# Compressed attention units of the second mixer: transposes three steps after their scores, first value product one step later

## The chip, the cores and the metric

The kernel runs on one core of one Trainium2 chip. The metric is the device time of one execution in microseconds. The core has TensorE (PE, its weight loads PEld), VectorE (DVE), ScalarE (ACT) and GpSimd (POOL), each with a queue of its own that is worked off in the order in which the program was written, and DMA queues. Engines wait for each other by semaphores.

## The reference, cut to what matters

The program is a block of several branches followed by a second block of two layers on a sequence of 1024 tokens of width 1024. The first layer of the second block has a mixer with three kinds of attention over the same queries, 8 heads in 2 groups of 4:

```
o_cmp, p_cmp = compressed_branch(q, kcmp, vcmp, slopes)   # 63 compressed tokens
idx = selection_indices(p_cmp, s)                         # per group, from p_cmp.sum over heads
o_sel = selected_branch(q, kv_heads(ks), kv_heads(vs), idx, slopes)
o_win = window_branch(q, kv_heads(kw), kv_heads(vw), slopes)
o = g[..., 0:1] * o_cmp + g[..., 1:2] * o_sel + g[..., 2:3] * o_win

# compressed_branch
logits = einsum('bgrtd,bgnd->bgrtn', q, kc) - slopes * dist
p = softmax(where(dist >= 0, logits, NEG)) * valid
o = einsum('bgrtn,bgnd->bgrtd', p, vc)
```

The window and selected branches are the same pattern with wider rows: scores, a bias by distance, exponentials, a product with the values, and a division by the row sum at the end. Only the compressed branch divides its probabilities before its value product, since their sum over heads also feeds the selection.

## The kernel before, in words

The attention of this mixer is cut into eight blocks of 128 queries, taken from the last (i = 7) to the first (i = 0). A block has 18 units: two compressed ones (kind "cmp", g = 0 and 1, four heads each, 4 x 63 columns), eight window units and eight selected units (kind "soft", one head each). A window unit is up to 640 keys wide (five blocks of 128; four or fewer from i = 3 on), a selected one up to 1024.

Each engine runs its own loop over steps, and a unit passes through them. In what follows S, T, C, P and O with a number stand for work of a block's unit of that number (0 and 1 are the compressed units, 2 the first window unit, 3 the second; -2 and -1 are the last two selected units of the block before).

- PE, per step: the scores S of the unit of this step (L1429 for cmp, L1435 for soft); the transposes T of the unit of two steps ago (L1453), 128 columns each; then value products: C0 for the first compressed unit three steps after its scores and C1 for the second five steps after (L1473), P for a pair of soft units (L1484); and O, the transposes of a finished group's output (L1494). L1503 are the transposes of a finished block.
- DVE, per step: the bias on the scores and the row minimum (L2866 cmp, L2875 soft); for a compressed unit of the step before the normalization, whose result T waits for (L2885, L2888, L2889, semaphore c_normed, then L2891, a sum over heads); the addition of finished outputs (L2902 for cmp; L2907, L2908 and four L2910 for soft); a part of the selection (L2630 to L2641) in six of the window steps.
- ACT, per step: the copies of transposed rows from PSUM to SBUF (L2112); the exponentials (L2098 cmp, L2102 soft); four steps after the last unit of a group the copy of its output (L2118), which O waits for.

T writes one of two PSUM banks in turn, so a transpose of piece t waits (n_copied) until ACT has copied piece t - 2. A row of more than four blocks of 128 has two pieces. C1 waits until DVE has added the output of group 1 of the block before (o_taken). The order on each engine is what the loops write; there is no planner. S of unit n waits until the bank it writes is free: for i of 4 and more that is after the bias of unit n - 2.

Of the kernel before, what the change touches and what calls it, by code (L numbers as in the profile page):

```python
# [67 lines left out]
def build(nc, x, c, w_mod, b_mod, g_pre, g_post, w_in, m_conv_w, m_conv_b, m_wq, m_wk, m_b_i, m_b_f,  # L68
# [5 lines left out]
    with ExitStack() as ctx:  # L74
# [437 lines left out]

        NSA_ORDER = list(range(TB - 1, -1, -1))

        def nsa_table():

            units, banks, pieces, turns, rows = [], [0] * 4, 0, 0, 0
            for o, i in enumerate(NSA_ORDER):
                for br, kind in enumerate(("cmp", "win", "sel")):
                    for h in range(0, N_H, 4 if kind == "cmp" else 1):  # L520
                        un = Unit()
                        un.kind, un.br, un.i, un.o, un.h, un.g, un.n = kind, br, i, o, h, h // 4, len(units)
                        un.b0 = max(0, i - 4) if kind == "win" else 0
                        un.blocks = 2 if kind == "cmp" else i + 1 - un.b0
                        un.w = 256 if kind == "cmp" else P * un.blocks
                        wide = 2 if i >= 4 else 1
                        bank_ = (un.n * wide) % 4
                        un.at = 512 * bank_
                        un.bank_free = max(banks[bank_:bank_ + wide])
                        banks[bank_:bank_ + wide] = [un.n + 1] * wide  # L530
                        un.first, un.last = un.h % 4 == 0, kind == "cmp" or un.h % 4 == 3
                        un.pieces = [(a, min(4, un.blocks - a)) for a in range(0, un.blocks, 4)]
                        un.piece = pieces
                        pieces += len(un.pieces)
                        un.row = rows
                        rows += kind != "cmp"
                        units.append(un)
            last_of = [max(un.n for un in units if un.o == o) for o in range(TB)]
            turn_of = []
            for step in range(len(units) + 10):  # L540
                if 0 <= step - 2 < len(units):
                    units[step - 2].turn = turns
                    turns += len(units[step - 2].pieces)
                if step - 8 in last_of:
                    turn_of.append(turns)
                    turns += 1
            soft = [un for un in units if un.kind != "cmp"]
            return units, soft, last_of, turn_of

        nsa_units, nsa_soft, nsa_last, nsa_turn = nsa_table()  # L550
        N_NSA = len(nsa_units)
# [416 lines left out]
        def _(pe):  # L968
# [471 lines left out]
            def n_turns(un):  # L1440

                if un.kind == "cmp":
                    pe.wait_ge(s.c_normed, 2 * un.o + un.g + 1)
                    row = crow[:, un.g, :]
                else:
                    pe.wait_ge(s.n_exp, un.row + 1)
                    row = ht[:, 4 + un.row % 4, :]
                for m, (a, blocks) in enumerate(un.pieces):
                    t = un.turn + m
                    if t >= 2:  # L1450
                        pe.wait_ge(s.n_copied, t - 1)
                    for b in range(blocks):
                        last = pe.transpose(ps[:, 2048 + 512 * (t % 2) + P * b:2048 + 512 * (t % 2) + P * b + P],  # L1453
                                            row[:, P * (a + b):P * (a + b) + P], ident[:, :])
                    last.then_inc(s.n_turned, 1)
# [12 lines left out]
            def c_values(un):  # L1468

                o = out_free(un)  # L1470
                pe.wait_ge(s.n_copied, un.turn + 1)
                for b in range(2):
                    last = mm(o[:, P * b:P * b + P], piece_of(un, b), vb[:, un.g, :], start=b == 0, stop=True,  # L1473
                              skip_group_check=True)
                last.then_inc(s.n_summed, 1)
# [32 lines left out]
            for step in range(N_NSA + 9):  # L1508
                if step < N_NSA:
                    n_scores(nsa_units[step])  # L1510
                if 0 <= step - 2 < N_NSA:
                    n_turns(nsa_units[step - 2])
                if at(step - 3, "cmp") and nsa_units[step - 3].g == 0:
                    c_values(nsa_units[step - 3])
                if at(step - 5, "cmp") and nsa_units[step - 5].g == 1:
                    c_values(nsa_units[step - 5])
                if at(step - 3, "soft") and nsa_units[step - 3].h % 2:
                    pair_values(nsa_units[step - 4], nsa_units[step - 3])
                if at(step - 5, "soft") and nsa_units[step - 5].last:
                    turned_out(nsa_units[step - 5])  # L1520
                if step - 8 in nsa_last:
                    n_heads(nsa_last.index(step - 8))
# [201 lines left out]
        def _(a):  # L1724
# [380 lines left out]
            def n_copies(un):  # L2105

                for m, (_, blocks) in enumerate(un.pieces):
                    t, p_ = un.turn + m, un.piece + m
                    a.wait_ge(s.n_turned, t + 1)
                    if p_ >= 8:  # L2110
                        a.wait_ge(s.n_summed, p_ - 7)
                    f(pt[:, 512 * (p_ % 8):512 * (p_ % 8) + P * blocks],  # L2112
                      ps[:, 2048 + 512 * (t % 2):2048 + 512 * (t % 2) + P * blocks], ACT.Copy).then_inc(s.n_copied, 1)
# [4 lines left out]
                f(out_t[:, un.g, :], bank(6 + un.g)[:, 0:256], ACT.Copy).then_inc(s.o_turned_in, 1)  # L2118

            for step in range(N_NSA + 9):  # L2120
                if 0 <= step - 2 < N_NSA:
                    n_copies(nsa_units[step - 2])
                if step < N_NSA:
                    n_exps(nsa_units[step])
                if step == N_NSA:
                    a.dma_start(xt[:, :, :], x_kept).then_inc(s.x_back, 16)
                if 0 <= step - 4 < N_NSA and nsa_units[step - 4].kind != "cmp" and nsa_units[step - 4].last:
                    out_taken(nsa_units[step - 4])
                if step - 8 in nsa_last:
                    i = nsa_last.index(step - 8)  # L2130
                    t = nsa_turn[i]
                    a.wait_ge(s.n_turned, t + 1)
                    f(no[:, :, P * NSA_ORDER[i]:P * NSA_ORDER[i] + P],
                      bank(4 + t % 2).rearrange("p (c t) -> p c t", c=4), ACT.Copy).then_inc(s.n_copied, 1)
# [217 lines left out]
        def _(v):  # L2352
# [563 lines left out]

            def outs_at(step):

                for n in (step - 4, step - 6):
                    if 0 <= n < N_NSA and nsa_units[n].last:  # L2920
                        un = nsa_units[n]
                        if n == step - 4 - 2 * (un.kind != "cmp" or un.g == 1):
                            n_outs(un)

            for step in range(N_NSA + 7):
# [632 lines left out]
```

## Time and profile before

| | us |
|---|---|
| runs (three) | 2985.83, 2989.27, 2983.74; median 2985.83 |
| profiled execution | 2981.65 |
| its span, first to last instruction | 2979.9 |
| PE busy | 2792.1 (94%) |
| DVE busy | 2028.3 (68%) |
| ACT busy | 1181.8 (40%) |
| mean granted TensorE clock | 0.97 |

The attention of the second mixer, the only place that the change touches, runs from about 902 to 1197 us of the span. The profile's slices 13 to 16 lie in it; PE is at 8 or 9 tenths there, DVE at 6 or 7. Shares of busy time say which engine is the fullest over the whole stretch, and not which one is late at a given place; for that the trace is read at one border between two blocks.

### The profile page before, as it was taken

The page shows a single profiled execution, that of the slowest core. Times are in us where ns is not written, and L with a number is a line of the kernel's source. Part 1 is how long each engine was busy: PE and PEld are TensorE (multiplying, and loading weights), DVE is VectorE, ACT ScalarE, POOL GpSimd, SP SyncE. Part 2 cuts the span into 40 slices and gives each one's busy share as a digit, 9 for nine tenths or more (in the row PEclk, how much of TensorE's full clock was granted, in tenths as well). Part 3 has the DMA queues.
Part 4 walks back from the last instruction along what each step waited for, and adds up shares of the span by engine and source line. Part 5 has one row for each costly group of instructions (what it writes and reads, how often), then busy time and mean ns, then how long its engine had stood idle before and what let it go on. Part 6 is the DMA issues. An engine that isn't in the chain of part 4 may idle for free.

```text
span 2979.9 us, 39880 instructions
## 1 busy us (share of the span) xinstructions
PE 2792.1 (94%) x15515; PEld 2271.9 (76%) x15515; DVE 2028.3 (68%) x3468; ACT 1181.8 (40%) x2129; POOL 82.4 (3%) x152
## 2 busy tenths in 40 slices
PE   3999999678998988999999999989989999999999
PEld 3868885467787876778888888878757788888887
DVE  5443417669536666478777777779984877776885
ACT  3333317543326776343333344421153433333444
POOL 1000000210040000000000000000000000000000
PEclk8999999999999998999999999999989999999999
DMA  7101200023200000333223383311002333335632
GB/s 308 36 25 29 64 24 15 5 75 112 64 26 1 1 1 1 134 102 117 105 105 108 126 293 96 92 43 50 23 16 74 104 106 113 113 113 201 219 99 99
DMA packets 185701, 256.29 MB, mean 86 GB/s; under 512 B 29575, under 2 KB 138539, under 8 KB 181035
## 3 DMA queue, kind: packets, MB, share of 16 engines
q1 hardware_dynamic: 181520, 232.45, 23.7%
q10 hardware_dynamic: 3995, 21.30, 1.8%
q8 instruction: 124, 2.03, 0.3%
q14 instruction: 62, 0.51, 0.1%
HBM read 186.62 MB, written 67.11 MB: 85 GB/s over the span
## 4 chain that ended last, share of the span: by engine, by line
PE 55%; DVE 3%; ACT 1%; DMA 0%; issue 0%; DVEq 0%; ACTq 0%
PE ps L1597 27%; PE ps L1605 14%; PE ps L1552 10%; PE ps L1661 2%; PE ps L1712 1%; PE ps L1698 0%; DMA ring<-in_ffn_w_gate_dram 0%; PE ps L1002 0%; DVE sc L2443 0%; DVE h_low L2447 0%; DVE w_ring L2974 0%; ACT big L2322 0%; ACT h_high L2340 0%; ACT sc L2343 0%; DVE x_ops L3084 0%
## 5 line engine op out<-in xcount | busy, mean ns | idle before, releaser
L1597 PE MATMUL ps<-x_ops,w_ring 128*128 128x512 f32 x3696 | 840.3, 389 | 6.3 <-ACT even_rows L2223 3.1
L1597 PEld LDWEIGHTS ps<-x_ops,w_ring 128*128 128x128 f32 x3696 | 693.2, 188 | 151.5 <-issue 7.8
L1605 PE MATMUL ps<-a_ring,w_ring 128*128 128x512 f32 x1848 | 419.6, 389 | 0.0
L1605 PEld LDWEIGHTS ps<-a_ring,w_ring 128*128 128x128 f32 x1848 | 346.7, 188 | 72.6 <-DVE w_ring L2974 0.7
L1552 PE MATMUL ps<-h_high,ring_parts 128*128 128x512 f32 x1024 | 320.3, 394 | 17.9 <-DVE h_low L2447 9.2
L2165 ACT ACTIVATE w_ring<-ring 128x512 fp32r<-128x512 f32 x230 | 144.1, 628 | 300.6 <-PE ps L1597 284.8
L1552 PEld LDWEIGHTS ps<-h_high,ring_parts 128*128 128x128 f32 x1024 | 193.4, 190 | 63.0 <-issue 12.7
L2456 DVE TENSOR_TENSOR ring_parts<-ring,ring_parts 128x1024 fp32r<-128x1024 f32 (+2 forms) x77 | 91.6, 1190 | 209.8 <-ACT ring_parts L1799 209.2
L1552 PE MATMUL ps<-h_low,ring_parts 128*128 128x512 f32 x512 | 200.7, 392 | 0.0
L1799 ACT ACTIVATE ring_parts<-ring 128x1024 fp32r<-128x1024 f32 (+2 forms) x77 | 76.0, 989 | 275.5 <-PE ps L1552 175.3
L2974 DVE TENSOR_TENSOR w_ring<-ring,w_ring 128x512 fp32r<-128x512 f32 x230 | 157.8, 686 | 38.8 <-ACT w_ring L2165 38.8
L2178 ACT ACTIVATE a_ring<-a_raw 128x512 fp32r<-128x512 f32 x150 | 94.6, 630 | 206.9 <-PE ps L1605 174.6
L2979 DVE TENSOR_TENSOR a_ring<-a_raw,a_ring 128x512 fp32r<-128x512 f32 x150 | 103.6, 691 | 95.0 <-ACT a_ring L2178 94.6
L1110 PE MATMUL ps<-h_high,ring_parts 128*128 128x512 f32 (+1 forms) x384 | 121.0, 396 | 6.8 <-DVE hin_low L2464 5.6
L1381 PE MATMUL ps<-h_high,ring_parts 128*128 128x512 f32 x384 | 121.7, 399 | 5.5 <-DVE nin_low L2745 4.2
L2165 ACT ACTIVATE w_ring<-late 128x512 fp32r<-128x512 f32 x100 | 62.9, 629 | 150.3 <-PE ps L1597 150.3
L1552 PEld LDWEIGHTS ps<-h_low,ring_parts 128*128 128x128 f32 x512 | 97.3, 190 | 20.4
L2112 ACT ACTIVATE sc<-ps 128x512 f32<-128x512 f32 (+3 forms) x208 | 87.9, 457 | 56.1 <-PE ps L1453 55.5
L1453 PE MATMUL ps<-ident,ht 128*128 128x128 f32 x560 | 92.1, 287 | 17.7 <-DVE ht L2889 17.0
L2102 ACT ACTIVATE ht<-ht,stat 128x640 f32<-128x640 f32 (+7 forms) x128 | 94.1, 736 | 26.7 <-DVE stat L2875 26.0
L1435 PE MATMUL ps<-kt,qt 128*128 128x512 f32 (+3 forms) x384 | 102.9, 380 | 0.0
L1147 PE MATMUL ps<-h_high,ring_parts 128*128 128x512 f32 (+1 forms) x288 | 94.6, 410 | 0.9 <-DVE ring_parts L2456 0.9
(478 smaller groups left out, 4636.6 us busy)
## 6 DMA issues: line engine op xcount, KB each, us to landing
a_raw<-act_kept SPq DMA_DIRECT2D x70, 512.0 KB, 3.8
act_kept<-even_rows SPq DMA_DIRECT2D x12, 1536.0 KB, 5.1
act_kept<-odd_rows SPq DMA_DIRECT2D x10, 1536.0 KB, 5.1
ring<-in_ffn_w_gate_dram SPq DMA_DIRECT2D x12, 1024.0 KB, 5.8
ring<-in_ffn_w_up_dram SPq DMA_DIRECT2D x12, 1024.0 KB, 6.0
ring<-in_conv_w_pw_dram SPq DMA_DIRECT2D x24, 512.0 KB, 3.9
late<-in_ffn_w_gate_dram SPq DMA_DIRECT2D x10, 1024.0 KB, 5.8
late<-in_ffn_w_up_dram SPq DMA_DIRECT2D x10, 1024.0 KB, 6.0
```

What stands on the lines that cost most here:

```text
L1110: last = mm(o[0:m, 512 * half:512 * half + 512], w(wp_, k), hin[rp_][:, k, 512 * half:512 * half + 512], start=k == 0 and p_ == 0, stop=k ...
L1147: last = mm(bank(o)[0:m, :], w(wp_, k), hin[rp_][:, k, 512 * (f % 2):512 * (f % 2) + 512], start=k == 0 and p_ == 0, stop=k == KC - 1 and ...
L1381: last = mm(o[:, 512 * half:512 * half + 512], w(wp_, k), nin_parts[rp_][k][:, 512 * half:512 * half + 512], start=k == 0 and p_ == 0, sto ...
L1435: last = mm(ps[:, un.at + a:un.at + a + e], q, kt[:, 4 * (un.br - 1) + 2 * part_ + un.g, k0:k0 + e], start=part_ == 0, stop=part_ == 1)
L1552: last = mm(bank(banks + half), (hi, lo)[wp_][:, k, :], h_part[rp_][:, k, 512 * half:512 * half + 512], start=k == order[0][0] and p_ == 0 ...
L1597: last = mm(o, w_ring[:, i % 4, wp_, P * k:P * k + P], x_ops[:, X_OP[p], rp_, k, :], start=p in "176" and k == 0 and p_ == 0, stop=k == 3 ...
L1605: last = mm(bank(OUT_BANK[DOWN_GROUP[p] + c_]), w_ring[:, (A_UNITS + b) % 4, wp_, P * c_:P * c_ + P], a_ring[:, b % 4, rp_, :], start=p in ...
L2102: f(row, row, ACT.Exp, bias=r[:, 0:1], scale=-1.0, accum_out=row_sums[:, un.row % 16:un.row % 16 + 1]).then_inc(s.n_exp, 1)
L2165: f(unit_part(i, 0), unit_raw(i), ACT.Copy).then_inc(s.u_hi, 1)
L2178: f(a_ring[:, b % 4, 0, :], x_down_raw(b), ACT.Copy).then_inc(s.x_hi, 1)
L2974: tt(unit_part(i, 1), unit_raw(i), unit_part(i, 0).bitcast(F32), sub).then_inc(s.u_split, 1)
L2979: tt(a_ring[:, b % 4, 1, :], x_down_raw(b), a_ring[:, b % 4, 0, :].bitcast(F32), sub).then_inc(s.x_split, 1)
```

## The change

The new function turned_in names the units whose transposes belong to a step: a compressed unit three steps after its scores, a soft one two steps after as before. The table of turns, PE's loop (n_turns) and ACT's loop (n_copies) use it. So in the step of unit 2 nothing is transposed, in that of unit 3 the first compressed unit, and in that of unit 4 the second compressed unit and unit 2. C0 comes four steps after its scores instead of three; C1 stays where it was. On DVE the addition of C0's output moves from the fourth to the fifth step. The turns keep their numbers and their banks.

```
+        def turned_in(units, step):
+            lags = ((3, True), (2, False))
+            return [units[step - n] for n, cmp_ in lags if 0 <= step - n < len(units) and (units[step - n].kind == "cmp") == cmp_]
...
-                if 0 <= step - 2 < len(units):
-                    units[step - 2].turn = turns
-                    turns += len(units[step - 2].pieces)
+                for un in turned_in(units, step):
+                    un.turn = turns
+                    turns += len(un.pieces)
...
                 if step < N_NSA:
                     n_scores(nsa_units[step])
-                if 0 <= step - 2 < N_NSA:
-                    n_turns(nsa_units[step - 2])
-                if at(step - 3, "cmp") and nsa_units[step - 3].g == 0:
-                    c_values(nsa_units[step - 3])
+                for un in turned_in(nsa_units, step):
+                    n_turns(un)
+                if at(step - 4, "cmp") and nsa_units[step - 4].g == 0:
+                    c_values(nsa_units[step - 4])
...
-                if 0 <= step - 2 < N_NSA:
-                    n_copies(nsa_units[step - 2])
+                for un in turned_in(nsa_units, step):
+                    n_copies(un)
                 if step < N_NSA:
                     n_exps(nsa_units[step])
...
-                for n in (step - 4, step - 6):
+                for n in (step - 5, step - 6):
...
-                        if n == step - 4 - 2 * (un.kind != "cmp" or un.g == 1):
+                        if n == step - 5 - (un.kind != "cmp" or un.g == 1):
```

PE at the border of the blocks i = 7 and i = 6, from T0 on, before:

```order
L1453 MATMUL ps<-ident,ht 128x128 [waits n_copied,c_normed]
L1453 MATMUL ps<-ident,ht 128x128
L1484 MATMUL ps<-sc,big 64x128 [waits n_copied]
L1484 MATMUL ps<-sc,big 64x128 x15
L1435 MATMUL ps<-kt,qt 128x512 [waits n_biased]
L1435 MATMUL ps<-kt,qt 128x512
L1435 MATMUL ps<-kt,qt 128x128 x2
L1453 MATMUL ps<-ident,ht 128x128 [waits n_copied,c_normed]
L1453 MATMUL ps<-ident,ht 128x128
L1473 MATMUL ps<-big,sc 128x128 [waits n_copied,o_taken0]
```

These are T0, P(-2,-1), S3, T1 and C0; S4, T2 and O(-1) follow. In the changed kernel, whose lines are five further on, the same place from S4 on:

```order
L1440 MATMUL ps<-kt,qt 128x512 [waits n_biased]
L1440 MATMUL ps<-kt,qt 128x512
L1440 MATMUL ps<-kt,qt 128x128 x2
L1458 MATMUL ps<-ident,ht 128x128 [waits n_copied,c_normed]
L1458 MATMUL ps<-ident,ht 128x128
L1458 MATMUL ps<-ident,ht 128x128 [waits n_copied,n_exp]
L1458 MATMUL ps<-ident,ht 128x128 x3
L1458 MATMUL ps<-ident,ht 128x128 [waits n_copied]
L1478 MATMUL ps<-big,sc 128x128 [waits n_copied,o_taken0]
L1478 MATMUL ps<-big,sc 128x128
L1499 MATMUL ps<-ident,ht 128x128 [waits o_turned_in]
```

P(-2,-1), S3 and S4 now stand ahead of T1; behind T1 come T2 in its two pieces, the second with a wait of its own, and only then C0, O(-1) and S5.

ACT at the same border, from the copy of T0 to the copy of T2, before:

```order
L2112 ACTIVATE sc<-ps 128x256 [waits n_summed,n_turned]
L2102 ACTIVATE ht,misc<-ht,stat 128x640 [waits n_biased]
L2112 ACTIVATE sc<-ps 128x256 [waits n_summed,n_turned]
L2102 ACTIVATE ht,misc<-ht,stat 128x640 [waits n_biased]
L2118 ACTIVATE ht<-ps 128x256 [waits n_summed]
L2112 ACTIVATE sc<-ps 128x512 [waits n_summed,n_turned]
L2112 ACTIVATE sc<-ps 128x128 [waits n_summed,n_turned]
```

and in the changed kernel:

```order
L2107 ACTIVATE ht,misc<-ht,stat 128x640 [waits n_biased]
L2117 ACTIVATE sc<-ps 128x256 [waits n_summed,n_turned]
L2107 ACTIVATE ht,misc<-ht,stat 128x640 [waits n_biased]
L2123 ACTIVATE ht<-ps 128x256 [waits n_summed]
L2117 ACTIVATE sc<-ps 128x256 [waits n_summed,n_turned]
L2117 ACTIVATE sc<-ps 128x512 [waits n_summed,n_turned]
L2117 ACTIVATE sc<-ps 128x128 [waits n_summed,n_turned]
```

The copy of T1 (the second 128x256 row) has moved behind the exponential of unit 3 and behind the output copy of the group before.

DVE at the same border, from the bias of unit 4 to that of unit 5, before:

```order
L2875 ISA ht,stat<-dists,ps 128x640 [waits n_turned,n_scored,dve_chain]
L2875 ISA stat 128x1
L2902 TENSOR_TENSOR ht<-ps,big 128x256 [waits n_summed]
L2634 TENSOR_TENSOR big<-big 128x16
L2635 MAX big<-big 128x8 [waits dve_chain]
L2636 MATCH_REPLACE big<-big 128x16 [waits dve_chain]
L2638 TENSOR_SCALAR big<-big 128x16 [waits dve_chain]
L2875 ISA ht,stat<-dists,ps 128x640 [waits n_turned,n_scored,dve_chain]
```

and in the changed kernel:

```order
L2639 TENSOR_TENSOR big<-big 128x16
L2640 MAX big<-big 128x8 [waits dve_chain]
L2641 MATCH_REPLACE big<-big 128x16 [waits dve_chain]
L2643 TENSOR_SCALAR big<-big 128x16 [waits dve_chain]
L2880 ISA ht,stat<-dists,ps 128x640 [waits n_turned,n_scored,dve_chain]
L2880 ISA stat 128x1
L2907 TENSOR_TENSOR ht<-ps,big 128x256 [waits n_summed]
L2912 RECIPROCAL big<-misc 128x4 [waits o_turned]
```

The addition of C0's output has moved behind the bias of unit 5, right ahead of the addition that C1 waits for (L2912 and what follows it). Nothing else moves on DVE.

## Rows read from the trace of the kernel before

**Rows 1.** Waits of PE, 900:1196: total us, times, longest us.

```profile
PE ps L1453 <- DVE ht L2889: 17.0, 16, 3.1
PE ps L1473 <- DVE ht L2910: 5.9, 7, 1.5
PE ps L1494 <- ACT ht L2118: 4.6, 8, 0.7
```

**Rows 2.** Timeline of PE, second border: start, us, what, [idle before <-releaser].

```profile
954.07 1.97 PE L1484 MATMUL ps<-sc,big 128*64 128x128 f32 x32
955.97 0.91 PE L1435 MATMUL ps<-kt,qt 128*128 128x512 f32 x4
957.36 0.44 PE L1453 MATMUL ps<-ident,ht 128*128 128x128 f32 x2 [0.49 <-DVE ht L2889]
957.64 0.61 PE L1473 MATMUL ps<-big,sc 128*128 128x128 f32 x4
958.00 0.88 PE L1435 MATMUL ps<-kt,qt 128*128 128x512 f32 x4
958.72 0.74 PE L1453 MATMUL ps<-ident,ht 128*128 128x128 f32 x5
960.07 0.44 PE L1494 MATMUL ps<-ident,ht 128*128 128x128 f32 x2 [0.61 <-ACT ht L2118]
960.26 0.88 PE L1435 MATMUL ps<-kt,qt 128*128 128x512 f32 x4
...
963.42 0.71 PE L1473 MATMUL ps<-big,sc 128*128 128x128 f32 x4 [0.30 <-DVE ht L2910]
```

**Rows 3.** Timeline of DVE, same border.

```profile
952.00 0.22 DVE L2866 CUSTOM_DVE_ANT_0 ht<-big,ps 128x63 f32<-128x63 f32 x1 [3.36 <-PE ps L1429]
...
955.49 0.81 DVE L2875 CUSTOM_DVE_ANT_0 ht<-dists,ps 128x640 f32<-128x640 f32 x1
...
957.97 0.82 DVE L2875 CUSTOM_DVE_ANT_0 ht<-dists,ps 128x640 f32<-128x640 f32 x1
...
960.12 0.42 DVE L2902 TENSOR_TENSOR ht<-ps,big 128x256 f32<-128x256 f32 x1
...
961.36 0.82 DVE L2875 CUSTOM_DVE_ANT_0 ht<-dists,ps 128x640 f32<-128x640 f32 x1
```

**Rows 4.** Timeline of ACT, same border.

```profile
956.35 0.83 ACT L2102 ACTIVATE ht<-ht,stat 128x640 f32<-128x640 f32 x1 [1.56 <-DVE stat L2875]
957.84 0.38 ACT L2112 ACTIVATE sc<-ps 128x256 f32<-128x256 f32 x1 [0.57 <-PE ps L1453]
958.83 0.83 ACT L2102 ACTIVATE ht<-ht,stat 128x640 f32<-128x640 f32 x1 [0.61 <-DVE stat L2875]
959.66 0.36 ACT L2118 ACTIVATE ht<-ps 128x256 f32<-128x256 f32 x1
```

**Rows 5.** Timeline of ACT, first block, exponential of unit 3.

```profile
912.86 0.83 ACT L2102 ACTIVATE ht<-ht,stat 128x640 f32<-128x640 f32 x1 [0.35 <-DVE stat L2875]
```

**Rows 6.** Timeline of PE, first block, unit 5.

```profile
914.85 1.52 PE L1435 MATMUL ps<-kt,qt 128*128 128x512 f32 x4
```

**Rows 7.** Timeline of DVE, last border, unit 4.

```profile
1174.19 0.29 DVE L2875 CUSTOM_DVE_ANT_0 ht<-dists,ps 128x128 f32<-128x128 f32 x1 [0.55 <-PE ps L1435]
```

**Rows 8.** Windows: stretch, busy of PE, PEld, DVE, ACT, POOL; clock, DMA, GB/s.

```profile
1111.00:1121.00 10.00, 6.25 (x50) 4.69 (x48) 9.28 (x44) 6.25 (x19) 0.00 (x0) 1.00 0.00 0
1142.00:1150.00 8.00, 4.27 (x37) 3.35 (x36) 7.21 (x35) 4.26 (x14) 0.00 (x0) 0.98 0.00 0
1150.00:1154.00 4.00, 4.00 (x24) 3.37 (x24) 1.79 (x8) 1.33 (x5) 0.00 (x0) 0.61 0.00 0
1154.00:1171.00 17.00, 13.95 (x126) 10.73 (x124) 11.79 (x70) 12.79 (x48) 0.00 (x0) 0.98 0.01 2
```

**Rows 9.** Timeline of PE: the same eight value matmuls at either clock.

```profile
1150.96 1.12 PE L1484 MATMUL ps<-sc,big 128*64 128x128 f32 x8
...
1154.14 0.66 PE L1484 MATMUL ps<-sc,big 128*64 128x128 f32 x8
```

## The prediction, made before the changed kernel was run

> **What bounds the kernel now.** The first view is the page's list of busy shares: PE is at 94%, so over the whole program any gap that is closed on PE is a gain. The second is the list of waits of PE inside the attention. It has one large entry: the transposes of the compressed units wait for DVE's normalization 16 times, 17.0 us together, up to 3.1 us [rows 1]. That is two waits in each of the eight blocks, at T0 and T1. Two smaller entries stand below it: C1 waits for DVE's addition of the block before, 5.9 us in 7 waits, and O waits for ACT's copy of an output, 4.6 us in 8 [rows 1]. The change aims at the first entry, so the third view must tell whether it is the one that ends last at a border.
>
> That view is the timeline of the three engines over one border, the one from 952 to 964 us. On DVE one wait opens it, 3.36 us before the biases of the second compressed unit at 952.00; after it the row at 961.36 and those before it have no wait at all [rows 3]. DVE works without a gap through two biases of compressed and three of window units, two normalizations, one addition and two parts of the selection. After the bias of unit 5 it does the addition of the last group, and that is what releases C1 at 963.42 [rows 2, 3]. In other borders the same is seen in coarse form: 9.28 us busy on DVE in 10, and 7.21 in 8 [rows 8]. So PE is the bound inside a block, but from S1 to C1 of each border it is DVE, and PE's waits at T0, T1, O and C1 are four places in which PE spends the same slack. C1 has a wait at each of the seven borders (5.9 us in 7, [rows 1]). A wait taken from T0 or T1 is handed on to C1 as long as DVE's row of work is as long as before.
>
> **What the change does to this row, at the borders of wide blocks (i = 6, 5, 4).** Nothing is added to DVE and nothing removed; only the addition of C0's output (0.42 us as printed; what follows starts 0.34 later) moves behind the bias of unit 5. I follow the border of [rows 2 to 4].
>
> PE: P(-2,-1), S3 and S4 no longer stand behind T0 and T1. In the old order P started at 954.07 and took 1.9 to the start of S3 at 955.97, S3 takes 0.75 (958.00 to 958.72 for the same shape less a little), T0 0.3, and S4 may start when the bias of unit 2 is done, 955.49 + 0.81 = 956.30 [rows 2, 3]. Even if P starts no earlier, S4 starts near 957.0 and ends near 957.7; if P starts 0.4 earlier, S4 is over before 957.36, when T1 is released by DVE. T1 is released at the same time as before, since DVE has done the same work up to then. So T1 runs at 957.36 to 957.7.
>
> ACT: the exponential of unit 2 starts at 956.35 and is over by 957.3, the copy of T0 follows at once, and T2's first piece can run at 957.7 to 958.2. Its second piece writes the bank of T1 and needs the copy of T1. Before, that copy ran at 957.84 [rows 4]. Now it stands behind the exponential of unit 3, which can't start before 958.83, as DVE gives the bias at 957.97 + 0.82 = 958.79, and behind the output copy at 959.66, whose successor starts 0.26 later, at 959.92 [rows 3, 4]. The copy of T1 then runs at 959.92 to 960.2, and T2's second piece starts at about 960.3. This is the new wait: some 2 us of PE, for ACT. What is queued behind it on PE: C0 (0.36, from 957.64 to 958.00), O(-1) (0.19, from 960.07 to 960.26) and S5 [rows 2]. S5 starts at 960.3 + 0.1 + 0.36 + 0.19 = 960.95 against 960.26 before.
>
> DVE: with the addition gone from its place it would reach the bias of unit 5 at 961.36 - 0.34 = 961.02. S5 takes 0.88 and ends at 961.83, with 0.05 for the signal (a T1 at 957.36 follows a normalization that ends at 957.31 by its own row) 961.9. So that bias is 0.5 later than before, the addition of C0's output comes behind it with 0.34, and the addition that C1 waits for is 0.5 + 0.34 = 0.85 to 0.9 later. PE gets to C1 before that and waits. Cost 0.9 us a border, for three borders 2.7 us. Bounds for one: not below -0.3 (if T2's second piece were not held up, S5 would be early, DVE would keep its length, and only what little waiting for scores it has could go) and not above +2.0 (the whole new wait on the path).
>
> **Narrow blocks (i = 3, 2, 1).** Here a window row has one piece, so T2 needs only the copy of T0, and the copy of T1 is next needed by unit 3, after S5. O(-1) still waits for the output copy behind the exponential of unit 3, a wait that all eight borders and the end have [rows 1], so S5 keeps its time. DVE comes to S5 0.34 earlier and then does the addition behind it: cost between 0 and 0.34. Where S5 was in time before by a few tenths the two cancel; I take 0.07 each, 0.2 together.
>
> **Last border (i = 0).** Here DVE had a real wait for S4, 0.55 us [rows 7]. S4 now stands ahead of T1 and this goes; S5 comes only little earlier, so I take 0.3 of it back: -0.3, bounds -0.55 and 0.
>
> **First block (i = 7).** There is no block before it, so no C1 wait to run into, and the 3.1 us of [rows 1] end with a normalization that waits for nothing that is moved. S3 goes into that wait, but T2's second piece again waits for the copy of T1, now behind the exponential that starts at 912.86 [rows 5]: 912.86 + 0.9 + 0.3 = 914.1, then 0.2 + 0.7 for the second piece and C0 at the low clock, and S5 at 915.0, against 914.85 [rows 6]. Cost +0.2, bounds -0.9 (one score group hidden) and +0.9.
>
> **Sum.** 3 x 0.9 + 0.2 - 0.3 + 0.2 = +2.8 us. Outside the span of 2979.9 lie 1.75 us that stay. The profiled execution took 2981.65 and would take 2984.5; the median of the three runs is 4.2 above the profiled one, so the forecast of a median is 2985.83 + 2.8 = 2988.6 us, +0.1%. What a measurement can tell of this kernel from no change is about 0.2%, 6 us: the likeliest finding is no difference. All seventeen microseconds of waits would be moved, not removed, and a little added.
>
> **Rivals.**
>
> A, the waits at T0 and T1 are worth what they show. PE is the fullest engine, and 17.0 us are gone: 2968.8; half of it, 2977.3. For it speaks only the share of 94%. Against it speak the C1 wait at all seven borders and DVE without a gap before it [rows 1, 3]. It would need DVE's row to be shorter, and it isn't. Chance 8%. (By the Trainium skill, page "Perfetto Trace Analysis", section "Optimization Strategy", one finds the gaps on the most contended engine and makes what blocks them start sooner or finish faster; applied to PE as the fullest engine this is rival A and 2968.8. The trace agrees that PE is the fullest over the whole, not that it is so at this place: the rule holds for the regime of interest, and in this one DVE is it.)
>
> B, no new wait. If the copy of T1 comes early enough all the same, the wide borders cost between 0 and +0.34 each, and the sum is about 0: 2986. For it: ACT is idle 1.56 and 0.61 us at this place [rows 4]. Against it: ACT's queue is in order, and the exponential ahead of the copy has a fixed time from DVE. Chance 12%.
>
> C, slower by the clock. At the border of i = 1, PE was busy 4.27 us in 8 and the clock, 0.98 there, was at 0.61 in the next 4 us; at the border of i = 2 it was busy 6.25 in 10 and the clock stayed at 1.00 [rows 8]. The changed order gathers the waits of T0 and T1 into one, with fewer transposes between. If the clock (levels 2.4 and 1.2 GHz) falls at the border of i = 2 too, or stays low through the whole block i = 1, that block is done at the lower level. The same eight value matmuls take 1.12 us there and 0.66 at full clock [rows 9], factor 1.7; the 13.95 us of PE in 1154 to 1171 become 23.7, more than the 17 us of the stretch, so +6.7 us, with the 2.8 of the sum +9.5: 2995.3. It decides from the point where the clock is still low at the first pair of block i = 1, and there PE and not ACT (12.79 of 17 us) becomes the bound. Chance 13%. (The Trainium skill, "TensorE: Matmul & The Clock Gate", section "A second HAM failure mode: psum-queue depth-cycling", says that frequent short idling between groups of matmuls lets the clock swing between its levels. The trace agrees in that two borders of eight show it.)
>
> **How the numbers follow.** Forecast 67%, A 8%, B 12%, C 13%. The likeliest one's own range is from +0.5 to +6: wide borders 3 x 0.3 at the least and 3 x 1.5 at the most, the rest within 1.5. The range for 8 of 10 takes in B and part of C, and the 2 to 3 us by which medians of few runs of this kernel wander (the three shown lie 5.5 us apart): 2982.5 to 2996. Faster by over 0.2%: 8%, all of A. Slower by over 0.2% (over 2991.8): C and the upper end of the forecast, 18%. Within: 74%.
>
> **What would show it.** Right: in the changed kernel PE's waits of L1458 for DVE are far below 17 us in number or length, new waits of L1458 for ACT's copies (L2117) stand at four places, the waits at L1478 for DVE's addition have grown, and the attention ends 2 to 4 us later. On DVE, the bias of unit 5 waits for PE at the wide borders. Wrong: the waits at C1 do not grow while the stretch is 10 us or more shorter (then DVE's row was not the bound); or the second piece of T2 has no wait (B); or the stretch is longer by more than 6 us with an unchanged clock, which would be a wait that I have not seen. If the granted clock of 1110 to 1200 differs from before, its part is told apart by comparing the wide borders alone, which lie at full clock.

## The result, and the profile after

| | before | changed |
|---|---|---|
| median of 20 runs each | 2983.65 us | 2988.84 us |
| lowest to highest | 2979.82 to 2989.27 | 2985.19 to 2995.71 |
| profiled execution, span | 2981.65, 2979.9 | 2986.13, 2984.4 |
| mean granted clock | 0.970 | 0.966 |

The ratio is 1.0015 with a 95% interval of 1.0008 to 1.0022: a small loss, 2.4 to 6.6 us. More runs of the kernel before were made beside it, so its median is 2.2 us lower than that of the three runs shown.

PE's waits from 900 to 1202 us in the changed kernel (total us, times, longest us); the first two answer to the first row of [rows 1], the others to its second and third:

```profile
PE ps L1458 <- DVE ht L2894: 9.4, 5, 3.0
PE ps L1458 <- ACT sc L2117: 8.8, 5, 2.0
PE ps L1478 <- DVE ht L2915: 5.1, 7, 1.2
PE ps L1499 <- ACT ht L2123: 3.3, 5, 1.2
```

By this list the waits of T0 and T1 for DVE have gone from 17.0 us in 16 to 9.4 in 5, and 8.8 us in 5 waits for ACT's copies are new. One of these five, 1.76 us at the border of i = 2, is put down to the wrong engine:

```profile
1122.86 0.42 DVE L2894 TENSOR_TENSOR ht<-ht,big 128x252 f32<-128x252 f32 x1
1123.33 0.76 PE L1458 MATMUL ps<-ident,ht 128*128 128x128 f32 x5 [1.76 <-ACT sc L2117]
```

The row of x5 starts with T1, which needs DVE's normalization (over at 1123.28) and not the copy that ACT made of T0 at the same time (over at 1123.29); the trace puts T1's weight load, at the same time, down to DVE (2.08 us). So the waits for DVE are 11.2 us in 6, and those for ACT 7.0 in 4: 0.87 in the first block and 2.05, 2.04 and 2.04 at the three wide borders. The 5.8 us taken from the first kind came back as 7.0 of the second: waits were moved, not removed.

The timeline of PE at the second border (start, us, what, [idle before <-releaser]), against [rows 2]:

```profile
956.05 1.97 PE L1489 MATMUL ps<-sc,big 128*64 128x128 f32 x32
957.95 0.90 PE L1440 MATMUL ps<-kt,qt 128*128 128x512 f32 x4
958.69 0.41 PE L1458 MATMUL ps<-ident,ht 128*128 128x128 f32 x2
958.85 0.89 PE L1440 MATMUL ps<-kt,qt 128*128 128x512 f32 x4
959.80 0.95 PE L1458 MATMUL ps<-ident,ht 128*128 128x128 f32 x6
962.79 0.33 PE L1458 MATMUL ps<-ident,ht 128*128 128x128 f32 x1 [2.05 <-ACT sc L2117]
962.96 0.62 PE L1478 MATMUL ps<-big,sc 128*128 128x128 f32 x4
963.41 0.38 PE L1499 MATMUL ps<-ident,ht 128*128 128x128 f32 x2
963.55 0.88 PE L1440 MATMUL ps<-kt,qt 128*128 128x512 f32 x4
...
966.95 0.71 PE L1478 MATMUL ps<-big,sc 128*128 128x128 f32 x4 [0.55 <-DVE ht L2915]
```

This border comes 2.43 us later in the trace than before (S1 at 953.33 against 950.90). T0 and T1 follow S3 and S4 without a wait; the row of x6 is T1 and the first piece of T2. The second piece of T2, x1, waits 2.05 us for ACT; it is called the held-up piece below. S5 starts at 963.55, that is 961.12 on the scale of before, against 960.26 [rows 2]: 0.86 late. C1 at 966.95 is 964.52 there, against 963.42: 1.1 late.

ACT in the same place, against [rows 4]:

```profile
958.78 0.83 ACT L2107 ACTIVATE ht<-ht,stat 128x640 f32<-128x640 f32 x1 [1.84 <-DVE stat L2880]
959.61 0.36 ACT L2117 ACTIVATE sc<-ps 128x256 f32<-128x256 f32 x1
961.27 0.83 ACT L2107 ACTIVATE ht<-ht,stat 128x640 f32<-128x640 f32 x1 [1.30 <-DVE stat L2880]
962.10 0.36 ACT L2123 ACTIVATE ht<-ps 128x256 f32<-128x256 f32 x1
962.36 1.07 ACT L2117 ACTIVATE sc<-ps 128x256 f32<-128x256 f32 x3
```

The copy of T1 is the first of the three in the last row. It stands behind an exponential that starts only when DVE has given its bias, and ACT is idle for 1.30 us, most of it with T1 ready to be copied (T1 is the first part of the row at 959.80).

DVE, against [rows 3]:

```profile
961.82 0.82 DVE L2880 CUSTOM_DVE_ANT_0 ht<-dists,ps 128x640 f32<-128x640 f32 x1
...
964.56 0.82 DVE L2880 CUSTOM_DVE_ANT_0 ht<-dists,ps 128x640 f32<-128x640 f32 x1 [1.13 <-PE ps L1440]
965.30 0.42 DVE L2907 TENSOR_TENSOR ht<-ps,big 128x256 f32<-128x256 f32 x1
```

The row of work that had no gap has one of 1.13 us ahead of the bias of unit 5, and the addition of C0's output now stands behind that bias.

**The borders one by one.** S1 of each border is found in PE's timeline; the length of a block is the distance from its S1 to the next one. Block i = 6, for example, is 994.61 - 950.90 = 43.71 before and 998.15 - 953.33 = 44.82 after:

```profile
950.90 1.06 PE L1429 MATMUL ps<-kc,qt 128*128 128x64 f32 x8
...
994.61 1.06 PE L1429 MATMUL ps<-kc,qt 128*128 128x64 f32 x8
```

```profile
953.33 1.06 PE L1434 MATMUL ps<-kc,qt 128*128 128x64 f32 x8
...
998.15 1.06 PE L1434 MATMUL ps<-kc,qt 128*128 128x64 f32 x8
```

Read so for every profile (block 7 from the first scores, block 0 to the last O; second profiles of both kernels included):

| us | 7 | 6 | 5 | 4 | 3 | 2 | 1 | 0 | sum |
|---|---|---|---|---|---|---|---|---|---|
| before | 48.57 | 43.71 | 41.74 | 40.37 | 33.25 | 28.93 | 26.96 | 29.20 | 292.7 |
| before, second profile | 48.06 | 43.73 | 41.73 | 40.38 | 33.25 | 28.94 | 26.19 | 29.19 | 291.5 |
| changed | 49.43 | 44.82 | 42.85 | 42.76 | 33.37 | 29.50 | 26.11 | 28.98 | 297.8 |
| changed, second profile | 49.49 | 44.83 | 42.82 | 42.75 | 33.37 | 29.42 | 26.09 | 28.97 | 297.7 |
| e1, copy ahead | 47.32 | 43.99 | 42.01 | 40.65 | 33.38 | 28.97 | 26.09 | 28.99 | 291.4 |
| e2, addition back | 48.76 | 44.79 | 43.40 | 41.44 | 33.27 | 29.25 | 25.76 | 28.79 | 295.5 |
| e3, both | 47.46 | 43.74 | 41.75 | 40.39 | 33.27 | 29.20 | 25.76 | 26.76 | 288.3 |
| e4, before, no head sum | 46.26 | 42.67 | 40.62 | 39.28 | 32.10 | 27.79 | 25.31 | 27.11 | 281.1 |
| e5, before, C1 later | 47.30 | 42.73 | 40.74 | 39.39 | 32.34 | 27.90 | 25.30 | 27.71 | 283.4 |
| e6, e3 with C1 later | 46.50 | 42.75 | 40.75 | 39.39 | 32.35 | 28.81 | 24.89 | 24.85 | 280.3 |
| e7, e3 with busy work | 46.72 | 43.72 | 41.75 | 40.38 | 33.25 | 28.93 | 26.81 | 25.64 | 287.2 |
| e8, e6 with busy work | 47.19 | 42.74 | 40.77 | 39.41 | 32.37 | 27.92 | 25.26 | 24.28 | 279.9 |
| e9, changed with busy work | 48.75 | 45.41 | 43.86 | 41.49 | 33.39 | 28.97 | 26.85 | 26.77 | 295.5 |

In the two kernels that were profiled twice, the columns 6 to 3 repeat within 0.03 us, which is much finer than the times of whole runs; the verdicts below rest on them. Every other kernel has one profile. The columns 7, 1 and 0 hold long stretches at the low clock and differ by up to 0.8 us between two profiles of one kernel.

Block 4 of the changed kernel is 2.39 us longer, not 1.1. The windows of that border (clock third from the end) show why:

```profile
1046.00:1050.00 4.00, 1.97 (x12) 1.29 (x10) 3.76 (x12) 2.25 (x6) 0.00 (x0) 1.00 0.00 0
1050.00:1054.00 4.00, 3.54 (x16) 3.35 (x17) 1.50 (x8) 1.98 (x6) 0.00 (x0) 0.57 0.00 0
```

PE's 2.04 us wait for ACT's copy ends at 1050.46, so most of it lies in the first stretch, and the granted clock is at the lower level, 1.2 GHz, in most of the second. The borders of i = 6 and 5 have the same wait (2.05 and 2.04 us) without a fall. In the kernel before the same border has no fall:

```profile
1035.00:1055.00 20.00, 17.05 (x161) 14.40 (x157) 14.63 (x55) 13.42 (x38) 0.00 (x0) 1.00 0.01 1
```

### The profile page after: what moved, and what is told of

The parts are those of the page before. It is cut to its first block, busy times and chain, and to the rows that moved or that the text cites. A ratio compares the mean times of both kernels' runs of the same rounds, so it can differ in the third digit from the quotient of the medians.

```text
span 2984.4 us, 39880 instructions
## 1 busy us (share of the span) xinstructions
PE 2797.1 (94%) x15515; PEld 2274.8 (76%) x15515; DVE 2028.6 (68%) x3468; ACT 1180.4 (40%) x2129; POOL 82.6 (3%) x152
## 4 chain that ended last, share of the span: by engine, by line
PE 55%; DVE 3%; ACT 1%; DMA 0%; issue 0%; DVEq 0%; ACTq 0%
PE ps L1602 27%; PE ps L1610 14%; PE ps L1557 10%; PE ps L1666 2%; PE ps L1717 0%; PE ps L1703 0%; PE ps L1007 0%; DMA ring<-in_ffn_w_gate_dram 0%; DVE sc L2448 0%; DVE h_low L2452 0%; DVE w_ring L2979 0%; ACT big L2327 0%; ACT h_high L2345 0%; ACT sc L2348 0%; DVE x_ops L3089 0%
## 5 line engine op out<-in xcount | busy, mean ns | idle before, releaser
L1458 PE MATMUL ps<-ident,ht 128*128 128x128 f32 x560 | 93.2, 291 | 19.2 <-DVE ht L2894 9.4
```

## The experiments

Each time is a median. The ratio is to the kernel before on the same chip, with its 95% interval; it is not the quotient of the medians, and differences in us are worked out from it.

**e1, ACT's copy of T1 ahead of the exponential of unit 3.** In the changed kernel's ACT loop:

```
-                for un in turned_in(nsa_units, step):
-                    n_copies(un)
+                for un in nsa_units[max(0, step - 3):step - 1] if step > 1 else []:
+                    if step - un.n == (3 if un.kind == "cmp" and un.g == 0 else 2):
+                        n_copies(un)
```

> The changed kernel, but ACT copies the transposes of the second compressed unit (T1) directly behind those of the first, ahead of the exponential of unit 3. Theory (DVE's row of work bounds a border, and the loss at wide borders is the second piece of T2 held up by that copy): the waits of the second piece of T2 for ACT, 2.0 us at four places in the changed kernel, are gone, S5 is back at its old time, and what is left of the loss is the addition of C0's output behind the bias of unit 5, at most 0.34 us a border: about +1.2 us against the kernel before, 3 to 4 us less than the changed kernel. Rival (the gathered idle time of PE lets the clock fall, and that is the loss): the time stays at +4 to +5 us, with clock dips at the same borders. Rival (the waits at T0 and T1 are worth what they show, and the copy hid it): -5 us or more against before.

Measured: 2983.64 us, ratio 1.0001 (0.9988 to 1.0013). The held-up piece is gone; what was x6 and x1 is one row of seven, and the only wait ahead of S5 is that of O for ACT:

```profile
961.49 1.24 PE L1458 MATMUL ps<-ident,ht 128*128 128x128 f32 x7
962.56 0.62 PE L1478 MATMUL ps<-big,sc 128*128 128x128 f32 x4
964.20 0.44 PE L1499 MATMUL ps<-ident,ht 128*128 128x128 f32 x2 [1.02 <-ACT ht L2123]
964.39 0.88 PE L1440 MATMUL ps<-kt,qt 128*128 128x512 f32 x4
...
967.80 0.71 PE L1478 MATMUL ps<-big,sc 128*128 128x128 f32 x4 [0.55 <-DVE ht L2916]
```

Blocks 6, 5 and 4 are 0.28, 0.27 and 0.28 us longer than before instead of 1.11, 1.11 and 2.39, and none of them has a fall of the clock. So the copy's place is 0.83 us of a wide border (1.11 - 0.28). What is left is under the 0.34 us of the addition's move. The interval of the time holds the +1.2 that was expected; the waits at T0 and T1 were changed here as in the changed kernel, and no 5 us came of it.

**e2, DVE's addition of C0's output back in the fourth step.** The changed kernel with before's outs_at:

```
-                for n in (step - 5, step - 6):
+                for n in (step - 4, step - 6):
...
-                        if n == step - 5 - (un.kind != "cmp" or un.g == 1):
+                        if n == step - 4 - 2 * (un.kind != "cmp" or un.g == 1):
```

> The changed kernel, but DVE adds C0's output in the fourth step as before, ahead of its part of the selection. Theory: C0 ends late at wide borders (behind the held-up piece), so DVE waits for it there about 0.7 us, in time that it would spend waiting for S5 anyway; the addition is off the row behind the bias of unit 5, so C1 is released about 0.3 us earlier at a wide border than in the changed kernel; in all +4 us against before, about 1 less than the changed kernel. If the addition's place were the whole loss: +1 or less. If it were nothing: as the changed kernel, +5.

Measured: 2988.09 us, ratio 1.0017 (1.0006 to 1.0029). Block 6 is 44.79, 1.08 longer than before: only 0.03 of the 0.3 came back. DVE did wait for C0, as expected, but what I had left out is that its part of the selection is queued behind the addition, so that this part no longer ran in the time of waiting for S5:

```profile
958.51 0.42 DVE L2907 TENSOR_TENSOR ht<-ps,big 128x256 f32<-128x256 f32 x1 [0.96 <-PE ps L1478]
...
959.75 0.82 DVE L2880 CUSTOM_DVE_ANT_0 ht<-dists,ps 128x640 f32<-128x640 f32 x1
```

The bias of unit 5 is now late by DVE's own row instead of by S5. With the held-up piece in place the addition's place is worth nothing; only without it (e1 against e3) is it worth 0.25. The two prices therefore do not simply add up: the copy's place is worth 0.83 with the addition moved (changed kernel against e1) and 1.05 with the addition back (e2 against e3). In this kernel the clock falls at the border of i = 5 (block 43.40) and not at that of i = 4 (41.44).

**e3, both.** The edits of e1 and e2 together; PE keeps the order of the changed kernel.

> The changed kernel with both of these undone: ACT's copy of T1 ahead of the exponential of unit 3, and DVE's addition of C0's output in the fourth step. PE's order is that of the changed kernel. Theory: DVE has the row of work of before with the arrivals of before, C1 is released at the old time at every border with 0.3 us gained at the last: 0 to -1 us against before, no difference that can be told, although the waits of T0 and T1 for DVE are moved. Rival (waits at T0 and T1 are worth what they show): -5 to -17 us. Rival (clock): slower than before by 1 us or more, with clock dips at borders where before had none.

Measured: 2979.70 us, ratio 0.9998 (0.9987 to 1.0009). Blocks 6 to 3 are 43.74, 41.75, 40.39 and 33.27, those of the kernel before within 0.03, although PE's waits at T0 and T1 are quite different (L1458 for DVE 9.4 us in 5, as in the changed kernel). What changed on PE's side is where the slack is spent:

```profile
958.42 0.44 PE L1499 MATMUL ps<-ident,ht 128*128 128x128 f32 x2 [1.02 <-ACT ht L2123]
...
961.76 0.71 PE L1478 MATMUL ps<-big,sc 128*128 128x128 f32 x4 [0.30 <-DVE ht L2916]
```

The wait at O is 1.02 instead of 0.61, that at C1 is 0.30 as in [rows 2]. At the narrow border of i = 2, however, the clock falls, which it does not in either profile of the kernel before, and block 2 takes 29.20 instead of 28.93 us:

```profile
1114.59 0.77 PE L1458 MATMUL ps<-ident,ht 128*128 128x128 f32 x5 [1.77 <-ACT sc L2117]
```

```profile
1115.00:1121.00 6.00, 4.96 (x28) 4.06 (x28) 5.18 (x25) 4.04 (x12) 0.00 (x0) 0.72 0.00 0
```

There T0 and T1 wait apart in the kernel before, 0.89 and 1.38 us; in the new order they are one wait of 1.77 (for DVE, as shown above for the changed kernel). This is the fall that the rival on the clock spoke of, at 0.27 us. The first and the last block are 1.1 and 2.4 us shorter in this one profile; these are the blocks that run largely at the low clock, and the timed runs do not tell the difference from none.

**e4, DVE's row made shorter.** The kernel before without the sum over heads; the selection works on zeros:

```
-                v.wait_ge(s.c_normed, n + 1)
-                chain(v.tensor_reduce(psum_p[:, un.g, 4:4 + N_CMP], row.rearrange("p r n -> p n r"), AX.X, add))
```

> The kernel before without DVE's two sums over heads per block (L2891, 0.59 us each, 0.62 from start to start); the selection then works on zeros. Nothing else is changed, PE and ACT have the order of before. Theory (DVE's row bounds a border from S1 to C1): 1.25 us less at each of seven borders and 0.6 in the first block, about -9 us. Rival (only PE's waits at T0 and T1 count): of these only T1 comes 0.62 earlier, -5 us at most. Rival (DVE is hidden): 0.

Measured: 2973.11 us, ratio 0.9965 (0.9953 to 0.9977), -10.4 us. Blocks 6 to 2 are 1.04, 1.12, 1.09, 1.15 and 1.14 shorter, for 1.24 us taken from DVE in each. PE's and ACT's orders were not touched. DVE, busy 68% of the whole span, sets the length of a border here. The rival's -5 lies outside the interval (-14.0 to -6.9), and its 0.62 a border lies well under what the blocks gave. Why the blocks gave 1.04 to 1.15 and not the whole 1.24 was not looked into.

**e5, C1 one step later.** The kernel before; in PE's loop:

```
-                if at(step - 5, "cmp") and nsa_units[step - 5].g == 1:
-                    c_values(nsa_units[step - 5])
                 if at(step - 3, "soft") and nsa_units[step - 3].h % 2:
                     pair_values(nsa_units[step - 4], nsa_units[step - 3])
+                if at(step - 6, "cmp") and nsa_units[step - 6].g == 1:
+                    c_values(nsa_units[step - 6])
```

and the counts of n_summed in ACT's copies and DVE's addition follow the new order of the products (C0, P(2,3), C1).

> The kernel before, with one move on PE: C1 comes one step later, behind P(2,3), S7 and T5. The counts by which ACT and DVE wait for value products are set to the new order; nothing else changes. Theory (from S1 to C1 the border is DVE's row, and C1 is where PE hands its slack back): P(2,3) no longer stands behind the wait for DVE's last addition, so what PE waited at C1 (5.9 us in 7) is regained as far as DVE is ready: 0.3 us at each of the first three borders and about 1 at the last four, together -4 to -6 us, with the 17 us of waits at T0 and T1 as large as before. Rival (only the waits at T0 and T1 count): 0.

Measured: 2971.26 us, ratio 0.9969 (0.9956 to 0.9981), -9.2 us, more than expected. The waits at C1 are gone, and those at T0 and T1 are nearly as large as before:

```profile
PE ps L1463 <- DVE ht L2899: 16.3, 16, 3.1
PE ps L1504 <- ACT ht L2128: 4.1, 7, 0.7
...
PE ps L1513 <- ACT sc L2122: 0.7, 3, 0.2
```

Each block from 6 to 3 is 0.91 to 1.00 shorter. In block 3 that is about the wait that C1 had (0.95); in the first three only 0.3 was waited there. The rest lies behind it. S7 comes earlier by the length of C1 as well, and DVE, which had stood idle for S7 ahead of the bias of unit 7 (first row, kernel before, 15.44 us after S1), goes on at once (second row, 14.56 after S1):

```profile
966.34 0.82 DVE L2875 CUSTOM_DVE_ANT_0 ht<-dists,ps 128x640 f32<-128x640 f32 x1 [0.90 <-DVE big L2641]
```

```profile
961.27 0.82 DVE L2885 CUSTOM_DVE_ANT_0 ht<-dists,ps 128x640 f32<-128x640 f32 x1
```

(The trace puts the 0.90 down to DVE's own instruction before it; S7, 965.30 to 966.20, ends later than that.) So the path of a block goes through DVE's row to C1 and then over C1, P(2,3) and S7 on PE back to DVE; e4 shortens its first part and e5 its second. The transposes of the finished block (L1513, L1503 before), which waited for ACT's copy of T5, come after more other work:

```profile
958.86 1.31 PE L1494 MATMUL ps<-sc,big 128*64 128x128 f32 x20
960.10 0.92 PE L1445 MATMUL ps<-kt,qt 128*128 128x512 f32 x4
960.85 0.73 PE L1463 MATMUL ps<-ident,ht 128*128 128x128 f32 x5
961.42 0.61 PE L1483 MATMUL ps<-big,sc 128*128 128x128 f32 x4
962.25 0.63 PE L1513 MATMUL ps<-ident,ht 128*128 128x128 f32 x4 [0.22 <-ACT sc L2122]
```

Their wait is 0.22 here and was 0.67 at each of the three wide borders of the kernel before. With the 0.30 of C1 that makes 0.75 of the 0.98 to 1.00; the remaining 0.25 was not taken apart.

**e6, e3 with C1 later.** Both orders together.

> The third experiment (changed kernel with ACT's copy ahead and DVE's addition back) with C1 one step later as well. Theory: the same gain as for the kernel before, -4 to -6 us against before at the borders, since the order of T0 and T1 gives nothing where DVE's row is the bound; where that row is no longer waited for (wide borders, which had 0.3 us at C1 and 0.6 at O), the later T0 and T1 may give up to 0.3 a border more. Rival: with C1 out of the way the waits of T0 and T1 become the limit, and this kernel is 3 us or more faster than the one with C1 alone moved.

Measured: 2972.43 us, ratio 0.9971 (0.9959 to 0.9982). Blocks 6 to 3 are those of e5 within 0.02. So with C1 out of the way, too, the later T0 and T1 give nothing; neither the 0.3 a border that I had allowed nor the rival's 3 us. Block 2 is longer than in e5 (28.81 against 27.90): as in e3, the clock falls at its border.

**e7, busy work in front of T0.** e3 with superfluous transposes that T0 overwrites, at the borders of i = 3 to 0:

```
-                    for b in range(blocks):
+                    for b in (0,) * 14 * (un.kind == "cmp" and un.g == 0 and un.i <= 3) + tuple(range(blocks)):
```

> The third experiment, with 14 superfluous transposes of the same 128 columns put in front of T0's own at the borders of i = 3, 2, 1 and 0 (about 1.3 us of PE each, into the bank that T0 writes right after; the result is the same). They fill PE's wait for T1 there. Theory of the border: PE's added work lies in a wait and costs nothing. If the clock's falls at these borders come with PE's idling, they go: the last block, 29.2 us in the kernel before and mostly at 0.50 of the clock, takes 26 to 27, so -2 to -4 us against the third experiment. If the clock falls for another reason: the same time as the third experiment or up to 2 us more.

Measured: 2980.60 us, ratio 0.9998 (0.9989 to 1.0008). Blocks 3 and 2 are 33.25 and 28.93, so the added PE work, 1.5 us at a border (T1's wait at i = 2 is 0.23 instead of 1.77), cost nothing there, and the fall at i = 2 is gone. The last block keeps the full clock from its border to about 1184, 2 us before its end, and takes 25.64 against 26.76 in e3 and 29.2 before:

```profile
1166.00:1183.00 17.00, 11.46 (x88) 8.36 (x86) 12.37 (x73) 10.89 (x47) 0.00 (x0) 1.00 0.00 1
```

But the whole run gained nothing that can be told from e3, so as a way to save time it is not shown.

**e8, e6 with the same busy work.**

> The sixth experiment (T0 and T1 as in the changed kernel, ACT's copy ahead, DVE's addition back, C1 one step later) with the superfluous transposes in front of T0 at the last four borders. Theory: what C1 gives (about 9 us) stays, the added work costs nothing, and the falls of the clock at these borders become fewer, so the last three blocks take 1 to 2 us less together than in the sixth (78.6 us there): -9 to -11 us against before. If the clock does not follow PE's idling: as the sixth, -8.6.

Measured: 2969.63 us, ratio 0.9961 (0.9946 to 0.9975), -11.6 us, the fastest kernel here by its median. Its interval overlaps those of e5 and e6, so what is shown is that it beats both the kernel before and the changed one, not that the busy work adds to it. In the one profile of each, the last three blocks take 77.5 us against 78.6 in e6, as expected; 0.9 of it is block 2, whose fall of the clock is gone.

**e9, the changed kernel with busy work,** at the borders of i = 4 to 0.

> The changed kernel itself with 14 superfluous transposes in front of T0 at the borders of i = 4, 3, 2, 1 and 0. If its block i = 4 (42.8 us in two profiles, 2.4 more than before) is made of 1.1 us from the held-up piece and 1.3 us from a fall of the clock, it takes 41.5 now; the last block, 29.0 us, takes 25.5 to 27; the borders of i = 6 and 5, untouched, stay at 44.8 and 42.8. In all 4 to 5 us less than the changed kernel, 0 to +1 against before. If the 1.3 us have another cause than the clock, block i = 4 stays at 42.8 or gets longer by the added work.

Measured: 2988.99 us, ratio 1.0018 (1.0007 to 1.0028). Block 4 is 41.49, as said: 1.12 us from the held-up piece, 1.27 from the clock. The last block is 26.77. The falls at i = 4 and 2 are gone, but others turned up at the borders of i = 6 and 5, which had none before and where nothing was edited; these blocks are 0.6 and 1.0 longer than in the changed kernel (45.41, 43.86):

```profile
960.00:963.00 3.00, 3.00 (x16) 2.72 (x14) 1.76 (x7) 1.81 (x5) 0.00 (x0) 0.62 0.00 0
1003.00:1009.00 6.00, 4.28 (x20) 4.01 (x21) 3.58 (x18) 3.69 (x11) 0.00 (x0) 0.72 0.01 4
```

So the expected gain in time did not come.

**Both kernels once more,** for a second profile each.

> The changed kernel once more, for a second profile of its borders. If the falls of the clock at the borders of i = 4 and i = 2, which its first profile has and the kernel before has not, belong to the kernel, they are at the same borders. If they are by chance, they are elsewhere, while the loss of 1.1 us at a wide border without a fall, and 0.9 in the first block, is there again.

> The kernel before once more, for a second profile: blocks of 43.7, 41.7, 40.4, 33.3 us for i = 6 to 3 again, and no fall of the clock at the borders of i = 4 and 2 if these belong to the changed kernel.

Measured: one execution each, 2991.05 and 2983.71 us. The blocks are in the table: the changed kernel repeats all eight within 0.08 us, its fall at i = 4 too. The kernel before repeats blocks 6 to 2 within 0.02 and has no fall at a wide border.

## Why the prediction was right

The forecast was 2988.6 us and no difference of over 0.2%; it came to 2988.84 and +0.15%. Part of the closeness of the first number is chance: the three runs of before lay 2.2 us above the median of twenty, and the loss is 5.2 us by the medians, where 2.8 was forecast.

- That the waits at T0 and T1 are not the limit: shown. e3 has the new order of PE and the old block lengths; e4 shortens DVE and the borders follow; rival A (2968.8) is out. What was moved was not all seventeen microseconds, as the sum had it, but 5.8.
- Wide borders, +0.9 each: measured +1.11 at i = 6 and 5. The chain was as described, link by link: the held-up piece starts at 960.36 on the scale of before (forecast 960.3), S5 0.76 behind it (forecast 0.65). e1 against the changed kernel makes the copy's part 0.83 (forecast 0.5 to 0.6), e1 against e3 the addition's 0.25 (forecast 0.34). S5's scores reach DVE 1.0 us after their start (963.55 to 964.56), not 0.93 as I took from their duration and one signal.
- That the waits at C1 would grow, one of the signs of being right, did not come out as a whole: 5.1 us in 7 against 5.9 before. They grew at i = 6 and 5 (0.30 and 0.29 to 0.55 and 0.56) and at i = 3 (0.95 to 1.06) and shrank at the others, most at i = 2 and 4, where the clock fell (1.23 to 0.35, 0.30 to 0.21).
- The wait at O was read too widely: it stands at six of the seven borders, inside block i = 1 and at the end, not at "all eight borders and the end". No term of the sum goes by it.
- Narrow blocks: i = 3 +0.12, forecast +0.07. Right.
- Last block -0.2, forecast -0.3: right in size, though mostly at the low clock in both, so it shows little.
- First block, forecast +0.2: the mis-sized term. Measured +0.86. S5 comes 12.76 us after the first scores (916.66 - 903.90) against 12.52 (914.85 - 902.33), which is the +0.24 that was forecast; the rest is that the clock rose later. From 918 to 922 the granted clock is 0.65 in the changed kernel; about 2.8 us are at the low level, so it rises some 16.9 us after the first scores, and by the same reading about 15.3 after them in the kernel before (0.80 in 916 to 920). That this belongs to the change is not shown: e9 has the same code in this block, its clock rises 15.3 after the first scores as before, and the block takes 48.75, 0.18 more than before.
- Rival C was right in kind and wrong in price. The clock did fall at borders that had no fall before: at i = 2, as C said, for about 0.5 us, and at i = 4, where I had not looked for it, for 1.3. It did not stay low through block i = 1, which is even 0.1 to 0.85 shorter, so the +6.7 us did not come. At the wide borders the falls go with the held-up piece: all four profiles with it (changed twice, e2, e9) have a fall at one or two of them, and all nine without it have none. At i = 2 they go with the one gathered wait of 1.8 us at T1: five of the six profiles with it (changed twice, e2, e3, e6; not e1) have a fall, and none of the three with busy work there (wait 0.23) or of the four with the old order (two waits).
- Rival B (copy early enough): false for the changed kernel, and made true by e1, whose sum of the blocks is 291.4.

By blocks, the loss of 5.1 us is 0.9 + 1.1 + 1.1 + 2.4 + 0.1 + 0.6 - 0.85 - 0.2, of which 3.3 are the held-up piece and the addition at three wide borders, and most of the rest goes with the clock. Against the second profile of the kernel before it is 6.3 us, as the clock-bound blocks 7 and 1 were shorter in that one.

## What to carry to other kernels

Closing a wait on the fullest engine gains nothing when that engine then waits just as long further on. Before closing one, look at the last wait of the stretch, here C1 behind DVE's addition, and ask whether the wait in front would only be handed on to it: e3 took 5.8 us from the largest waits and gained nothing that can be told, e5 left them nearly as they were and gained 9. When a step is moved on one engine, list what its follower now stands behind on the other engine's in-order queue; here ACT's copy of T1 fell behind an exponential with a fixed time. And move the instruction that hands the slack back (e5) rather than the one that shows the largest wait.

## What the runs showed of the hardware that was not expected

A wait of PE of 2.0 us at a wide border, with only shorter ones near it, went in some places with a fall of the granted clock to 1.2 GHz for about 3 us (0.57 over 1050 to 1054), and in others with none. The price was 1.3 us at i = 4 of the changed kernel and 0.6 to 1.0 elsewhere (e2, e9). Which of the three wide borders it was depended on the kernel (i = 4 in the changed one, i = 5 in e2, i = 6 and 5 in e9) and was the same in the two profiles of the changed kernel. In e9, work added to keep PE busy at some borders was followed by falls at others. At i = 2, two waits of 0.9 and 1.4 us of PE went with the full clock in four profiles of four, one wait of 1.8 us with a fall in five of six, and busy work in that wait with the full clock in three of three. What decides the place at the wide borders was not settled.
